# A router that reads x before the norm's division, and expert buffers placed anew, in a hybrid decoder step with top-2-of-8 experts

## What is computed

```python
x = x + jnp.concatenate([y_ssd, y_lru], axis=-1) @ P['w_out'][l]
hn = rmsnorm(x, P['ln_ffn'][l])          # x * rsqrt(mean(x*x) + EPS) * gain
x = x + moe_swiglu(hn, P['moe_w_router'][k], ...)

def moe_swiglu(x, w_r, wg, wu, wd):      # wg, wu: 8 x 1024 x 3584, wd: 8 x 3584 x 1024
    logits = (x @ w_r).astype(jnp.float32)
    top_v, top_i = lax.top_k(logits, TOP_K)
    gates = jax.nn.softmax(top_v, axis=-1)
    dense_gate = jnp.sum(jax.nn.one_hot(top_i, N_EXPERTS, dtype=jnp.float32) * gates[..., None], axis=-2)
    for e in range(N_EXPERTS):
        out = out + dense_gate[..., e:e + 1] * swiglu(x, wg[e], wu[e], wd[e])
```

## Time and profile before

| | us |
|---|---|
| median of 3 runs | 1793.11 (1790.26 to 1794.79) |
| profiled execution | 1795.45 |
| its span, first to last instruction | 1793.8 |
| PE busy | 1729.1 (96%) |
| DVE busy | 1363.6 (76%) |
| ACT busy | 1051.6 (59%) |
| mean granted clock of TensorE | 0.986 of full speed |

### The profile page before, as it was taken

How to read it: one execution, slowest core, us unless ns; L and a number is a source line. 1 busy time by engine, 2 the same in 40 slices (tenths; PEclk the granted TensorE clock), 3 DMA queues, 4 the chain that set the end, 5 groups by cost and what they waited for, 6 DMA issues and landing times.

```text
span 1793.8 us, 24165 instructions
## 1 busy us (share of the span) xinstructions
PE 1729.1 (96%) x9024; PEld 1450.5 (81%) x9024; DVE 1363.6 (76%) x1387; ACT 1051.6 (59%) x1006; POOL 111.6 (6%) x119
## 2 busy tenths in 40 slices
PE   7999999999999998899999999999999999999995
PEld 5877899999787788788788788788788787887884
DVE  3679756664366964688888888888988888888885
ACT  2535544443334453476767776776766777776763
POOL 2054000000115300000000000000000000000000
PEclk9999999999999999899999999999999999999998
DMA  8455355646445444399899899899999998998990
GB/s 249 141 190 176 121 163 165 188 130 200 154 130 192 163 142 134 129 364 358 318 356 352 320 358 351 324 352 343 335 355 321 352 357 307 369 352 315 362 357 32
DMA packets 257027, 465.45 MB, mean 259 GB/s; under 512 B 8492, under 2 KB 108196, under 8 KB 256928
## 3 DMA queue, kind: packets, MB, share of 16 engines
q1 hardware_dynamic: 250288, 442.20, 71.5%
q0 software_dynamic: 6384, 21.28, 3.5%
q10 hardware_dynamic: 288, 1.08, 0.2%
HBM read 453.70 MB, written 11.15 MB: 259 GB/s over the span
## 4 chain that ended last, share of the span: by engine, by line
PE 88%; DVE 7%; ACT 2%; issue 2%; DMA 0%; ACTq 0%; DVEq 0%; POOL 0%; POOLq 0%
PE bank L847 85%; PE bank L851 3%; DVE arena L1637 2%; DVE w_lo L1640 1%; DVE moe_arena L1637 1%; ACT arena L1310 1%; DVE fw_lo L1640 1%; ACT fw_hi L1310 1%; DVE cs_t L1640 0%; DVE arena L1640 0%; DVE sam_y L1723 0%; ACT ysb_hi L1310 0%; DMA arena<-in_x_sample 0%; DVE bank L1845 0%; DVE ysb_lo L1637 0%
## 5 line engine op out<-in xcount | busy, mean ns | idle before, releaser
L1640 DVE TENSOR_TENSOR w_lo<-wring,w_hi 128x2048 fp32r<-128x2048 f32 x336 | 768.3, 2291 | 118.1 <-ACT w_hi L1310 117.1
L1310 ACT ACTIVATE w_hi<-wring 128x2048 fp32r<-128x2048 f32 x336 | 643.4, 1918 | 254.5 <-PE bank L847 254.4
L847 PE MATMUL bank<-w_hi,xg_hi 128*128 128x512 f32 x896 | 359.6, 401 | 10.7 <-DVE w_lo L1640 9.0
L847 PE MATMUL bank<-w_lo,xg_hi 128*128 128x512 f32 x896 | 355.0, 396 | 0.0
L847 PE MATMUL bank<-w_hi,xg_lo 128*128 128x512 f32 x896 | 352.6, 394 | 0.0
L847 PE MATMUL bank<-hn,wring 128*128 128x264 f32 x1152 | 269.1, 391 | 8.5 <-DVE hn L1637 6.1
L847 PEld LDWEIGHTS bank<-hn,wring 128*128 128x128 f32 x1152 | 218.6, 192 | 51.5 <-issue 11.7
L847 PEld LDWEIGHTS bank<-w_hi,xg_hi 128*128 128x128 f32 x896 | 168.3, 188 | 51.2 <-DVE w_lo L1640 12.6
L847 PEld LDWEIGHTS bank<-w_lo,xg_hi 128*128 128x128 f32 x896 | 168.2, 188 | 40.9
L847 PEld LDWEIGHTS bank<-w_hi,xg_lo 128*128 128x128 f32 x896 | 168.4, 188 | 38.7
L847 PE MATMUL bank<-w_hi,at_hi 128*128 128x512 f32 x448 | 178.8, 399 | 0.0
(11 more groups left out here) (242 smaller groups left out, 2077.7 us busy)
## 6 DMA issues: line engine op xcount, KB each, us to landing
wring<-in_moe_w_gate SPq DMA_DIRECT2D x112, 1024.0 KB, 5.2
wring<-in_moe_w_up SPq DMA_DIRECT2D x112, 1024.0 KB, 5.2
wring<-in_moe_w_down SPq DMA_DIRECT2D x112, 1024.0 KB, 5.0
wring<-in_w_in SPq DMA_DIRECT2D x36, 1024.0 KB, 5.4
wring<-in_w_out SPq DMA_DIRECT2D x16, 1024.0 KB, 5.3
wring<-in_ffn_w_gate SPq DMA_DIRECT2D x11, 1024.0 KB, 5.4
wring<-in_ffn_w_up SPq DMA_DIRECT2D x11, 1024.0 KB, 5.4
wring<-in_ffn_w_down SPq DMA_DIRECT2D x16, 704.0 KB, 4.7
```

Source lines behind the costliest of these rows:

```text
L847: return nc.tensor.matmul(out, lhsT, rhs, start=start, stop=stop)
L1310: return nc.scalar.activation(out, in_, fn, **kw)
L1640: return V.tensor_tensor(out, in0, in1, op)
```

## The change

The mean of squares is no longer taken for all tiles at the end. In layer 1 DVE multiplies each finished tile of `xT` with the gain into `hn` (`weigh_tile`), as it did in layer 0, and sums the squares of tiles 0 to 6 (`add_square`). PE takes up router matmuls and token transposes within the output projection: k tiles 0, 1 behind step 4, 2 and 3 (with the transposes of tiles 0 to 3) behind step 5, 4 and 5 between tiles 6 and 7 of step 7, 6 and 7 at the end. The mean of squares comes as one number per token (`mean_squares`, bank BN); ACT takes its root into `rstd`, DVE the reciprocal. `rstd` scales the eviction of `hntok`, the samples' columns and the Exp of the gates. The first job's `sel_m` comes straight from `position` and `picked` (`select`), and gates and tables stand behind the gather and behind the split of unit 2. ACT splits units 0 and 1 in steps 6 and 7, DVE unit 0 in step 6. Transposes of `xT` are spread between other work and over other banks. `w_hi` and `w_lo` are six tensors of one unit each, placed one by one over arrays of the mixers; the other buffers of the stage move as well. The zeroing of `sct` moves from ahead of `choose(0)` to the memsets of `ysb_hi` and `ysb_lo`.

```diff
+XTOKF = ((BA, 0, 0), (BB, 1, 0), (BN, 2, 0), (BA, 0, 1), (BB, 1, 1), (Q0, 2, 1))
...
-        w_hi, w_lo = (sb(n, [P, SPLITS, UNIT], F32R) for n in ("w_hi", "w_lo"))
+        w_hi, w_lo = ([split_places[f"w_{part}{i}"] for i in range(SPLITS)] for part in ("hi", "lo"))
...
+            def logits(k):
+                out = begin("logits") if k == 0 else bank[fill("logits")[0]]
+                pe.wait_ge(hn_ready, 24 + k + 1)
+                for t in range(3):
+                    ins = mm(out[:, t * NE:(t + 1) * NE], hn[:, k, TOK0[t]:TOK0[t] + P], w_router[:, k, :],
+                             start=k == 0 and t == 0, stop=k == KD - 1 and t == 2)
+            def token_rows(k):
+                h = k // 4
+                for t in range(2):
+                    out = begin("hntok", t, h) if k % 4 == 0 else bank[fill("hntok", t, h)[0]]
+                    ins = flip(out[:, k % 4 * P:(k % 4 + 1) * P], hn[:, k, TOK0[t]:TOK0[t] + P])
+            def mean_squares():
+                out = begin("ms")
+                pe.wait_ge(sq_ready, 16 + 8 + KD)
+                pe.wait_ge(sum_square, KD - 2)
+                for t in range(3):
+                    mm(out[:, t:t + 1], rs[:, 1, cols], mean_d[:, 0:1], start=True, stop=False)
+                    mm(out[:, t:t + 1], last[:, cols], mean_d[:, 0:1], start=False, stop=True)
+                mm(out[:, 3:3 + NB], mean_d[:, :], rs[:, 1, TP:T], start=True, stop=False)
+                done(mm(out[:, 3:3 + NB], mean_d[:, :], last[:, TP:T], start=False, stop=True), "ms")
...
+                        if l == 1 and m == KD - 1 and not lru:
+                            for k in (4, 5):
+                                logits(k)
+                                token_rows(k)
...
-                if l == 1:
-                    ln_ffn()
...
+            logits(6)
+            token_rows(6)
+            residual_rows(0, 0)
+            logits(7)
+            token_rows(7)
+            mean_squares()
+            residual_rows(1, 0)
+            residual_rows(2, 0)
+            residual_rows(0, 1)
             out = begin("rank")
...
+            residual_rows(1, 1)
+            residual_rows(2, 1)
...
+            keep_residual(0, 0)
+            evacd(f(rstd[:, :], filled("ms")[:, 0:3 + NB], ACT.Sqrt, bias=eps[:, :]), "ms")
+            keep_residual(1, 0)
+            act.wait_ge(rstd_ready, 1)
+            for h in range(2):
+                for t in range(2):
+                    evacd(f(hntok[:, t, 512 * h:512 * h + 512], filled("hntok", t, h)[:, :], scale=rstd[:, t:t + 1]),
+                          "hntok", t, h)
...
+            filled("gather", 1)
+            high_part(1)
+            split(0, 2, first=True)
+            keep_residual(2, 1)
+            act.wait_ge(max_ready, 1)
             for t in range(3):
+                f(ex[:, t, :], ex[:, t, :], ACT.Exp, scale=rstd[:, t:t + 1]).then_inc(lexp_ready, 1)
...
+            tt(cmp_a[:, :, :, :], l_f, l_e, ALU.is_gt)
+            link(tt(cmp_b[:, :, :, :], l_f, l_e, ALU.is_equal))
...
+            stt(picked[:, :, :], picked[:, :, :], 1.5, over(valid[:, :], NE), ALU.is_lt, ALU.mult).then_inc(picks_ready, 1)
+            evacuated("ms")
+            V.reciprocal(rstd[:, :], rstd[:, :]).then_inc(rstd_ready, 1)
...
+            select(lambda t: position[:, t, 0:1], lambda t: picked[:, t, 0:1])
+            split(0, 1)
...
+            for i in range(2):
+                dve.wait_ge(xg_hi_ready, i + 1)
+                evacd(low_slots(i, filled("gather", i)), "gather", i)
+            split(0, 2)
+
+            dve.wait_ge(lexp_ready, 3)
             link(tt(gates[:, :, :], ex[:, :, :], picked[:, :, :], ALU.mult))
...
-            choose(0)
-            for p in range(1, SPLITS):
-                split(0, p)
...
+            V.memset(sct[:, :, :].bitcast(F32), 0.0)
             V.memset(ysb_hi[:, :].bitcast(F32), 0.0)
             V.memset(ysb_lo[:, :].bitcast(F32), 0.0).then_inc(y_free, 1)
```

More of the change, by code:

```diff
@@ L183, in plan_fills @@
     pl.add(Q0, "logits")
[L184 to L188, removed]
+    for h in range(2):
+        for t in range(2):
+            pl.add(Q1 + 2 * h + t, "hntok", t, h)
+    pl.add(BN, "ms")
     pl.add(Q0, "rank")
+    for b, t, h in XTOKF:
+        pl.add(b, "xtokf", t, h)
     for i in range(2):
@@ L1120, in _ @@
                         ins.then_inc(half_used, 1)
+                    if l == 1 and OUT_ORDER[q] == (1, 0):
+                        for k in (0, 1):
+                            logits(k)
+                    if l == 1 and OUT_ORDER[q] == (3, 1):
+                        for k in (2, 3):
+                            logits(k)
+                        for k in range(4):
+                            token_rows(k)
                 def ln_ffn():
@@ L1320, in high_weights, with used, split @@
                 f(hi, w).then_inc(fhi_ready, 1)
+            def used(j, p):
+                if p < 0:
+                    j, p = j - 1, p + PER_JOB
+                mat, s, h = STREAM[p]
+                n = j * STEPS + s + 1
+                if h == 0:
+                    act.wait_ge(split_used, j * (PER_JOB // 2) + p // 2 + 1)
+                elif mat == "d":
+                    act.wait_ge(down_done, n)
+                else:
+                    b = G_BANK if mat == "g" else U_BANK
+                    act.wait_ge(full[b], moe0[b] + n)
+            def split(j, p, first=False):
+                if not first:
+                    used(j, p - SPLITS)
+                slot = p % RING
+                act.wait_ge(w_landed[slot], 16 * (landed0[slot] + j * (PER_JOB // RING) + p // RING + 1))
+                f(w_hi[p % SPLITS][:, :], wring[:, slot, :]).then_inc(hi_ready, 1)
             load_tokens(act)
@@ L1477, in scaled_high @@
                             f(hn_hi[:, k], hn[:, k]).then_inc(hn_hi_ready, 1)
+                    if l == 1 and q == len(OUT[l]) - 2:
+                        act.wait_ge(hrows_out, LAYERS * 32)
+                        states_stored(act, LAYERS - 1)
+                        split(0, 0, first=True)
                     if q == len(OUT[l]) - 1:
@@ L1481, in _ @@
                             scaled_high(3)
+                        else:
+                            split(0, 1, first=True)
+                            f(ssum[:, 0:1], eps[:, :], ACT.Sqrt)
                         out_squares()
@@ L1536, in split @@
[L1536 to L1547, removed]
@@ L1549, in _ @@
+            act.wait_ge(xs_normed, 1)
             xs = hn[:, :, TP:T]
             f(xg_hi.rearrange("p i (q s) -> p (i q) s", s=P)[:, :, SLOTS:P], xs).then_inc(xs_ready, 1)
-            for t in range(3):
[L1552 to L1559, removed]
+            keep_residual(0, 1)
@@ L1990, in _ @@
                                    ).then_inc(hid_lo_ready, 1)
[L1993 to L2000, removed]
+            V.memset(sel_m[:, :, :], 0.0)
             out = filled("logits")
```

204 lines of the change are left out of this document (116 added, 88 removed).

## The result

The changed kernel takes 1764.76 us (median of 4 runs, 1763.48 to 1768.95), the kernel before 1793.95 us beside it (4 runs, 1790.26 to 1795.6): a ratio of 0.9847, 95% interval 0.9831 to 0.9862, or 29.2 us less. The prediction said 1778, range 1769.5 to 1786.

A forecast was written before the change was run, and what follows sets the result against it. PE was taken to bound nearly all the time, with a routing relay leaving it idle or slow. 16.45 us gained to unit four less 1.7 for a second clock fall gave 14.75 us less: 1778 us, range 1769.5 to 1786.

The forecast's parts named there:

- Steps (1) to (5): From projection to unit four: standstill removed, added router work, picks, clock and gather, late DVE queue; gain 16.45 us.
- The standstill: PE's 5.81 us idle behind the mean of squares, during root, reciprocal and products, was to leave the path.
- Step (4): Behind the projection the clock falls near 711 and returns within the gather, which takes 5.0 us, bounds 3.8 and 6.9.
- rival A: Clock stays at 2.4 GHz through the routing; unit four starts 21.4 us sooner, 1772 us; chance 0.20.
- Step (6): PE's 2.35 us wait before unit four brings a second clock fall, costing 1.7 us, bounds 0 and 3.4.
- Step (7): Expert buffers' new places cost nothing, as splits are the same instructions at other places.
- this stage keeps its length: The eight expert jobs, from 753.20 us on with PE never free, were to last as long as before.
- Rival C: New places slow the splits, so DVE bounds all 336 units; at 2.72 us a split 1802 us; chance 0.04.
- B: More waits in the projection or first job, or a clock fall there, each 1.7 to 3 us; 1785 us; chance 0.13.
- D: Expert stage bound by loads, so an earlier start ends in waits for weights; no change, 1791 us; chance 0.05.

The follow-up runs named there:

- router last: Changed kernel with router matmuls and token transposes of k tiles 0 to 5 behind the output projection instead of within it; 1770.05 us, run again 1774.4 us.
- 32 bytes later: Changed kernel with the six expert split buffers, sct and the small routing arrays moved up by 32 bytes; 1778.82 us, ratio 0.9908.
- 64 bytes later: Changed kernel with its six unit buffers moved by 64 bytes, still on multiples of 64; median 1769.94 us, ratio 0.9873.
- the places alone: Kernel before with the changed kernel's buffer places and sct memset place, its old order of work kept; 1784.44 us against 1794.77, ratio 0.9942.
- changed, again: The changed kernel itself, nothing edited, timed again beside the router-last edit on the same chip; 1765.1 us, ratio 0.9845.
- memsets on GpSimd: Changed kernel with the three memsets of sct, ysb_hi and ysb_lo moved from DVE to GpSimd; 1764.95 us, ratio 0.9854.
- the ring moved: Changed kernel with the three memsets on GpSimd and the ring of landed units 32 bytes later, on a multiple of 64; 1763.93 us, ratio 0.9847.

## Why the prediction was right in sign and too small

**Steps (1) to (5): right.** The standstill is gone. The work within the projection was taken at 5.4 us and is 5.2. On the axis of before, logits were to be full 29.1 us behind the mark and are at 28.7; the picks take 2.2 us for 2.4; the gather 5.12 for 5.0; from it to the first product 1.53 for 1.55. Unit four was to wait 2.35 us behind table switch, tables and memsets, and waits 2.53. The table switch, taken at 1.283 us, took 1.28, or 1.75 with the 0.47 us of "issue" just ahead of it. The gain to unit four was to be 16.45 us; it is 17.43 in both profiled executions of the changed kernel, against the one trace before.

**Step (4), the clock: right in these two executions, and no fixed quantity.** It falls at 708.2, which is 710.7 on the axis of before (the mark lies 2.5 us later there), where the forecast had 711, and it comes back within the gather, as forecast; PE did not stand ahead of the fall. But the same program had 3.4 and 17.1 us at 1.2 GHz in two executions (router last), and the order of work of the change had 10.2 in three (with 32 bytes later) and none in one (64 bytes later). So my forecast and rival A are not alternatives: both occur, execution by execution, 4.2 us apart (55.03 and 50.83). That step (4) came out to the microsecond is partly luck. The Trainium skill (TensorE: Matmul & The Clock Gate, What's actually happening) says that activity releases the throttle. The rows agree only in part: PE's records fill 705 to 725 in the second execution of the router last while the clock is at its lower level for most of it (0.59 and 0.55).

**Step (6), a second fall: wrong, 1.7 us too dear.** 719 to 735 has a clock of 1.00 around a 2.53 us wait.

**Step (7), "the new places: nothing": wrong, and this is the step that failed.** It asked only whether the splits get longer, since they write into those buffers. PE reads them, in 512-column products that fill the eight jobs, and there the places are worth 0.8 us a job, 6.6 us in all. The same error stands at the prediction's start, "this stage keeps its length". Without the 6.6 us the kernel would have come out at 1771.4, inside the range. Rival C had the same blind spot. Both the places alone (127.66) and their loss by 32 bytes (128.57) show it. The Trainium skill (SBUF — State Buffer, Who interferes with whom) says of PE and ACT that they "never wait on anyone", which is said of other engines' access to SBUF and not of where an operand lies. No run here measures such a wait; the places do change the spacing of PE's products, whatever the mechanism.

**The sum.** 14.75 us forecast; 1.0 more to unit four, 1.7 not lost, 6.6 from the places make 24.1, which is 1771 on the profiled execution before (1795.45 - 24.1). The measured median is 6.6 us lower still, which only by chance is the same number as that of the places. Of it 2.4 are the shorter front ahead of the mark, in which nothing was changed, and 4.2 are what the profiled execution after took above its median. Against the median before, 1793.95, the unexplained rest is 5.1, as the profiled execution there was 1.5 above it. For its cause there is evidence and no proof. Time and mean granted clock of single runs, the profiled one first:

| kernel | runs |
|---|---|
| changed | 1768.95 at 0.990; 1765.12 at 0.992, 1763.48 at 0.995, 1764.4 at 0.994 |
| changed, again | 1771.9 at 0.990; 1766.6 at 0.992, 1765.1 at 0.992, 1764.42 at 0.994, 1764.23 at 0.993 |
| 64 bytes later | 1759.5 at 0.994; 1770.24 at 0.988, 1767.92 at 0.989, 1769.94 at 0.989, 1770.3 at 0.988 |
| 32 bytes later | 1778.9 at 0.990; 1774.17 at 0.993, 1778.73 at 0.990, 1779.33 at 0.990 |

Within a kernel a run with a clock lower by 0.003 to 0.006 is some 4 to 11 us longer. The two profiled runs of the changed kernel are its slowest; 4.2 us less is what a relay at the full clock gives. But in which stretch the unprofiled runs had the higher clock isn't known: in the traces it is low ahead of the mark too, for 3.4 to 10.2 us by execution. It also means that medians of such kernels differ by several us through the draw alone, so I rest on the traces for the parts.

**The rivals.** B (more waits) and D (loads bound) didn't happen: PE is full through the projection, and ACT's splits still wait for PE, 249.5 us. The clock of A occurred in one execution of the order of the change, and in both with the memsets on GpSimd. Missing among them was a gain in the stage that I had taken to keep its length.

No version beat the changed kernel by more than its runs spread; the one with memsets on GpSimd and the ring moved has 1763.93 us.

## What to carry to other kernels

When buffers move, ask of every engine that reads or writes them, above all of the one that bounds the longest stage: a change of 1.6 ns on average in products that follow each other after 237 ns was worth 6.6 us here, over a third of the 17.4 that the rebuilt relay gave. Measure such a side effect apart, with the old order and the new places. And where one trace shows the clock low for ten microseconds, take that as one draw: a forecast should carry the execution with and without it as its own spread, not as a rival.

## What the runs showed of the hardware

The spacing of 512-column products depends on where their operands lie in SBUF. Jobs take 127.52, 127.53 and (in seven traces of one layout) 127.63 to 127.69 us in three layouts, and 128.41, 128.44, 128.47 and 128.57 in four others, and within a trace all six jobs agree to 0.1 us. Moving the buffers by 32 bytes costs 0.94 us a job in one layout; in the other it changes the job by 0.06, no more than two executions of the changed kernel differ (127.63 and 127.69).

TensorE's clock fell to 1.2 GHz in stretches where its records left no gap (10.00 us busy of 10.00 at 0.59), made of products 8 or 1 columns wide and transposes, and how long it stayed there differed by up to 14 us between executions of the same program (3.4 and 17.1).
